# FFN down product of a decoder step as a seven-product Strassen form with standing weights

## What is computed

```python
    y = (jax.nn.silu(gc) * (xn @ w_up)) @ w_down
    return y, gb[:, t:]
...
        yp = yp + f
```

## Time and profile before

| | us |
|---|---|
| median of 3 runs | 2670.74 (2669.45 to 2671.27) |
| the profiled execution | 2667.81 |
| its span, first to last instruction | 2665.9 |
| TensorE busy | 2372.2 (89%) |
| VectorE busy | 1158.6 (43%) |
| ScalarE busy | 675.4 (25%) |
| GpSimd busy | 640.3 (24%) |
| mean granted TensorE clock | 0.953 of full speed |

### The profile page before, as it was taken

The page is one execution under the profiler, slowest core; times in us unless marked ns, Lnnn a source line. Parts: engine busy times, 40 slices in busy tenths (PEclk is TensorE's granted clock), DMA queues, the critical chain, the costliest instruction groups (busy, mean ns, idle before and its releaser), DMA issues. The chain is left out here.

```text
span 2665.9 us, 32803 instructions
## 1 busy us (share of the span) xinstructions
PE 2372.2 (89%) x12653; PEld 1606.8 (60%) x12673; DVE 1158.6 (43%) x2482; ACT 675.4 (25%) x1660; POOL 640.3 (24%) x710
## 2 busy tenths in 40 slices
PE   6999997876888788688779798889999999999999
PEld 4644444553555455455534345458888888878888
DVE  4479997870466566644413112244334433400000
ACT  2321113445455354344401014211111111100000
POOL 1020221113565455456401010022222221100000
PEclk9999997997999899899989899989999999999999
DMA  3211101005899688555430303111111111041100
GB/s 130 72 60 69 37 1 40 1 1 194 303 335 339 242 326 310 180 161 165 118 144 1 110 0 127 64 66 48 33 49 48 33 49 48 18 162 56 58 14 15
DMA packets 125549, 281.75 MB, mean 106 GB/s; under 512 B 14181, under 2 KB 59796, under 8 KB 125396
## 3 DMA queue, kind: packets, MB, share of 16 engines
q0 software_dynamic: 49408, 176.19, 19.5%
q1 hardware_dynamic: 74788, 99.15, 10.9%
q10 hardware_dynamic: 1200, 4.33, 0.4%
HBM read 261.55 MB, written 17.94 MB: 105 GB/s over the span
## 5 line engine op out<-in xcount | busy, mean ns | idle before, releaser
L595 PE MATMUL PS<-X,XT 128*128 128x512 f32 (+5 forms) x864 | 330.5, 538 | 4.3 <-DMA X<-w_in 4.3
L595 PEld LDWEIGHTS PS<-X,XT 128*128 128x128 f32 (+1 forms) x864 | 154.3, 183 | 166.6 <-issue 140.9
L1797 ACT COPY X<-PS 128x512 f32<-128x512 f32 x352 | 193.5, 592 | 213.5 <-PE PS L1678 127.3
L839 DVE TENSOR_SCALAR_CACHE_REDUCE mask<-score,cand 128x384 bf16<-128x384 f32 (+2 forms) x198 | 181.5, 942 | 3.2
L2070 PE MATMUL PS<-dn_w,H 128*128 128x256 f32 x704 | 155.5, 383 | 5.3 <-DMA dn_w<-w_down 5.3
L2070 PE MATMUL PS<-XT,H 128*128 128x256 f32 x704 | 153.3, 380 | 0.0
L2070 PEld LDWEIGHTS PS<-dn_w,H 128*128 128x128 f32 x704 | 134.8, 192 | 25.9 <-DMA dn_w<-w_down 5.7
L2097 DVE TENSOR_TENSOR X<-PS,X 128x256 f32<-128x256 f32 (+1 forms) x36 | 15.2, 423 | 309.4 <-PE PS L2070 308.9
L2070 PEld LDWEIGHTS PS<-XT,H 128*128 128x128 f32 x704 | 133.4, 190 | 19.6 <-issue 0.8
L1550 POOL DMA_INDIRECT XT<-cache_b_v,gather_b x128 | 120.0, 938 | 88.8 <-PE PS L1761 51.4
L1761 PE MATMUL PS<-XT,sa_pt 128*32 128x512 f32 (+1 forms) x1024 | 84.9, 462 | 25.8 <-DMA XT<-cache_b_v,gather_b 19.3
(11 more groups left out here) (408 smaller groups left out, 4415.4 us busy)
## 6 DMA issues: line engine op xcount, KB each, us to landing
ffn_wg<-w_gate SPq DMA_DIRECT2D x11, 1024.0 KB, 5.2
ffn_wu<-w_up SPq DMA_DIRECT2D x11, 1024.0 KB, 5.2
X<-w_in SPq DMA_DIRECT2D x4, 2048.0 KB, 7.8
XT<-w_down SPq DMA_DIRECT2D x2, 2816.0 KB, 16.7
X<-x_prompt ACTq DMA_DIRECT2D x8, 512.0 KB, 7.2
wo_w<-w_out SPq DMA_DIRECT2D x4, 1024.0 KB, 9.6
X<-x_prompt SPq DMA_DIRECT2D x8, 512.0 KB, 13.0
mem_keys<-cache_mem_k SPq DMA_DIRECT2D x8, 512.0 KB, 4.8
```

The source lines that it names most:

```text
L595: last = nc.tensor.matmul(M.PS[0:n, s % 3, 0:chunks[j].width], XT[:, c, t * P:t * P + n], w[:, j % 2, c, 0:chunks[j].width], start=(c == 0 ...
L839: self.link.send(nc.vector.tensor_scalar(self.mask[:, sc], self.score[:, sc], as_float[:, x:x + 1], 0.0, op, ALU.add, accum_out=self.count ...
L1797: nc.scalar.copy(dst, M.PS[0:dst.shape[0], T0 + x % 2, 0:dst.shape[1]]).then_inc(t_read, 1)
```

## The change

`residual_stage` goes and `down_stage` takes its place. Nothing else in the program is changed, except that X and XT are now two parts of one tile named `region`, so that sums of 5808 elements a partition can lie across both.

- The operands change places. Blocks of 11 x 128 x 128 weights stand in the array, and 264 tokens of H move. The 22 feature slices are split into even and odd, the tokens into two halves of 528, and the output columns into pairs of 128. A pair is a 2 x 2 block product, done as seven products in place of eight, each for two pieces of 264 tokens: 14 groups of 11 matmuls to a pair, 4 pairs. The semaphore `mm` counts these groups.
- VectorE makes four sums of H (t1 to t4) once, at the stage's start; t3 is written over a block of H.
- GpSimd makes four sums of weight blocks for each pair: s1 = a21 + a22, s2 = s1 - a11, a21 = a11 - a21, a12 = a12 - s2, each of 1408 elements a partition.
- Weights come as blocks of 128 columns, so in runs of 512 bytes. SyncE issues the four of the first pair; ScalarE issues those of the next pair between its copies.
- Each product block has features on the partitions. TensorE turns it back by five transposes per output quarter (`turn`), 16 turns in all; VectorE adds PSUM to the residual piece in `rest` (`finish`).
- The residual is read from `x_scratch` in pieces of 128 columns, two or three transfers each, and stored the same way; a piece is loaded after the store that used its half of `rest`.

```diff
-def residual_stage(nc, M, K, name, lhs, kc, w_dram, ncol, store=None, spare=None, spilled=None):
...
+def down_stage(nc, io, M, K, H, region):
+    HT = NTOK // 2
+    TW = HT // 2
+    KH = FT // 2
+    PAIRS = KC // 2
+    A, D2, C, TB, TE = 0, 2, 4, 6, 7
...
+        slots = S.sb("w", [P, 6, KH, P])
+        p1, u2, u3, c21 = (S.sb(n, [P, HT]) for n in ("p1", "u2", "u3", "c21"))
+        rest = S.sb("rest", [P, 2, 5, P])
+        t1, t2, t4 = (region[:, k * KH * HT:(k + 1) * KH * HT].rearrange("p (k n) -> p k n", k=KH) for k in range(3))
...
+        t3 = b12
...
+            @block_.sync
+            def _(sp):
+                for i in range(4):
+                    sp.dma_start(block(0, i), weights(0, i)).then_inc(a_loaded[i], 16)
...
+                load(0)
+                load(1)
+                for z in range(4 * PAIRS):
+                    sp.wait_ge(y_done, z + 1)
+                    store(z)
+                    if z + 2 < 4 * PAIRS:
+                        sp.wait_ge(stored[z % 2], 16 * len(stretches(z)) * (z // 2 + 1))
+                        load(z + 2)
...
+            @block_.gpsimd
+            def _(pool):
+                for q in range(PAIRS):
+                    a11, a12, a21, a22, s1, s2 = (block(q, i) for i in range(6))
+                    pool.wait_ge(a_loaded[2], 16 * (q + 1))
+                    pool.wait_ge(a_loaded[3], 16 * (q + 1))
+                    if q:
+                        pool.wait_ge(mm, 14 * (q - 1) + 12)
+                    nc.gpsimd.tensor_tensor(s1, a21, a22, ALU.add).then_inc(w_summed, 1)
+                    pool.wait_ge(a_loaded[0], 16 * (q + 1))
+                    if q:
+                        pool.wait_ge(mm, 14 * q)
+                    pool.wait_ge(w_summed, 4 * q + 1)
+                    nc.gpsimd.tensor_tensor(s2, s1, a11, ALU.subtract).then_inc(w_summed, 1)
+                    nc.gpsimd.tensor_tensor(a21, a11, a21, ALU.subtract).then_inc(w_summed, 1)
+                    pool.wait_ge(mm, 14 * q + 4)
+                    pool.wait_ge(w_summed, 4 * q + 2)
+                    nc.gpsimd.tensor_tensor(a12, a12, s2, ALU.subtract).then_inc(w_summed, 1)
...
+            @block_.tensor
+            def _(pe):
+                def product(bank, left, right, x, begin):
+                    for c in range(KH):
+                        last = nc.tensor.matmul(M.PS[:, bank + x, 0:TW], left[:, c, :],
+                                                right[:, c, x * TW:(x + 1) * TW], start=begin and c == 0,
+                                                stop=(c == KH - 1), skip_group_check=not begin)
+                    last.then_inc(mm, 1)
+
+                def turn(z, src):
+                    if z:
+                        pe.wait_ge(y_done, z)
...
+                        last = nc.tensor.transpose(out, src[:, a - first:a - first + n], K("ident"))
+                    last.then_inc(turned, 1)
...
+                    pe.wait_ge(w_summed, 4 * q + 2)
+                    if q == 0:
+                        pe.wait_ge(x_summed, 2)
+                    for x in range(2):
+                        pe.wait_ge(copied, 6 * q + x + 1)
+                        product(A, s2, t2, x, False)
...
+            @block_.scalar
+            def _(act):
...
+                    for x in range(2):
+                        act.wait_ge(mm, 14 * q + 8 + x + 1)
+                        copy(u3, x, A, copied)
+                    if more:
+                        load_next(q, 2)
+                        load_next(q, 3)
...
+            @block_.vector
+            def _(dve):
+                nc.vector.tensor_tensor(t1, b12, b11, ALU.subtract).then_inc(x_summed, 1)
+                dve.wait_ge(x_summed, 1)
+                nc.vector.tensor_tensor(t2, b22, t1, ALU.subtract).then_inc(x_summed, 1)
+                nc.vector.tensor_tensor(t3, b22, b12, ALU.subtract).then_inc(x_summed, 1)
+                dve.wait_ge(x_summed, 2)
+                nc.vector.tensor_tensor(t4, b21, t2, ALU.subtract).then_inc(x_summed, 1)
...
+                finish(4 * PAIRS - 2)
+                finish(4 * PAIRS - 1)
...
+        region = sb(ctx, "region", [P, NT * D + KC * NTOK])
+        M.X = region[:, 0:NT * D].rearrange("p (t d) -> p t d", t=NT)
+        M.flat = region[:, NT * D:NT * D + KC * NTOK]
...
+        down_stage(nc, io, M, K, H, region)
```

More of the change, by code:

```diff
@@ L2890, in build @@
         Stage.stores = {n: ctx.enter_context(nc.semaphore(n)) for n in (
-            "in_store_done0", "in_store_done1", "kv_store_done0", "kv_store_done1", "ffn_stored0", "ffn_stored1", "dn_stored")}
+            "in_store_done0", "in_store_done1", "kv_store_done0", "kv_store_done1", "ffn_stored0", "ffn_stored1", "dn_stored0", "dn_stored1")}
         M.PS = ctx.enter_context(nc.psum_tensor("PS", [P, 8, 512], F32))
@@ L2896, in build @@
         M.mem_loaded = ctx.enter_context(nc.semaphore("mem_loaded"))
-        M.X = sb(ctx, "X", [P, NT, D])
-        M.XT = sb(ctx, "XT", [P, KC, NTOK])
-        M.flat = M.XT[:].rearrange("p k n -> p (k n)")
+        region = sb(ctx, "region", [P, NT * D + KC * NTOK])
+        M.X = region[:, 0:NT * D].rearrange("p (t d) -> p t d", t=NT)
+        M.flat = region[:, NT * D:NT * D + KC * NTOK]
+        M.XT = M.flat.rearrange("p (k n) -> p k n", k=KC)
         ncst = max(o + w for n, (_, o, w) in const_at.items() if not for_setup(n))
```

156 lines of the change are left out of this document (added).

## The result

| | before | after |
|---|---|---|
| median, us | 2670.09 (2668.34 to 2671.27) | 2635.15 (2632.86 to 2636.51) |
| ratio | | 0.9869, 95% interval 0.9852 to 0.9886 |
| the profiled execution | 2667.81 | 2636.51 |
| its span | 2665.9 | 2634.7 |
| start of the down product | 2338.27 | 2339.42 |

The change is faster by 34.9 us, 1.3%. 28.2 us were forecast, and the time is 1.9 us under the low end of the range. The direction was right, and so was the mechanism in the main; the gain was larger than forecast.

What follows compares the result with a forecast made beforehand. TensorE's matmul columns were taken as the bound: products, clock and turns 287.6 us against 320.8, 33.2 us less; with 0.65 and 4.4 us lost, 28.2 us less. Forecast 2642.5 us, range 2637 to 2652 us.

Steps and rivals of the forecast that it cites:

- The products: TensorE's matmuls in the down product: 1232 records of 0.2225 us, 274.1 us.
- The turns: Five transposes after product blocks: 0.8 us each, 11.2 us for 14; bounds 0.65 and 1.7 us a turn.
- The clock at the start: TensorE's first records in the stage run at a lower clock, costing 2.25 us.
- The start, 0.65 us lost: First weight block of the stage lands at 4.7 us instead of 4.04 us, so TensorE starts 0.65 us later.
- The end, 4.4 us lost: Behind the last product, turn, sums and stores take 7.1 us instead of 2.7 us.
- Rival 1: Stage start: fourth block lands behind 12.65 us, t3 goes first, TensorE waits 5.5 us; 2648.0 us, chance 0.27.
- Rivals 2 and 4: Turns between products: 1.7 us each, about 2657 us, chance 0.08; or they lower TensorE's clock, 2684.4 us, chance 0.03.
- Rival 3: Weights late at each change of pair: three waits of 5 us each, 2657.5 us, chance 0.05.
- The taking of turns between VectorE and GpSimd: Sums at the stage's start: each engine waits for the other's whole instruction; s2 ready at 25.85 us, 0.6 us early.
- The landing of the fourth block, 11.9 us: Last weight block of the first pair lands 11.9 us into the stage, bounds 10.1 to 12.9 us.
- the price of a packet: Weight loads at the stage's start: 28 ns for a packet of 512 bytes, bounds 23 and 31 ns.

Runs made afterwards that it cites:

- e_plain8: The changed kernel with eight block products and no sums in place of seven products: ratio 1.0011 to the kernel before, stage 335.3 us.
- e_turns2: The changed kernel with each turn's five transposes done twice: ratio 0.9916 to the kernel before, stage 304.1 us.
- e_region: The kernel before with X and XT as two parts of one tile and nothing else: ratio 0.9995 to the kernel before, stage 327.4 us.
- a_after: The changed kernel run again, unaltered, on another chip: 2770.45 us against 2804.03 for the kernel before, ratio 0.9868, stage 302.2 us.
- e_late_guard: The changed kernel with the first pair's fourth block issued behind the residual pieces and VectorE waiting for s1 before t3: ratio 0.9884 to before, stage 295.3 us.
- e_split_swap: The changed kernel with the first block in two transfers and s1's product ahead of s2's: ratio 0.9867 to the kernel before, stage 294.1 us.
- e_late: The changed kernel with the first pair's fourth block issued behind the five residual pieces: ratio 0.9883 to the kernel before, stage 302.1 us.

## Why the prediction was off

- **The products**: right. 274.1 us forecast; 283.46 less the turns' 7.6 and the clock's 1.7 leaves 274.2. The price from the FFN stage carried over, and e_plain8 shows the count to be the lever.
- **The turns, "0.65 us for five. I add 0.15 us"**: the step that failed most. They take 0.55 us each, so 11.2 us were forecast for the 14 on the path and 7.6 measured: 3.6 us too dear. The burst of eight in 1.04 us already contained the last record's whole duration; in the chain only the distance between starts counts, 0.11 us, and the break that had 0.15 us costs nothing (e_turns2). The lower bound was the burst's price, so it lay above the truth too.
- **The clock at the start**: 2.25 us forecast, 40.83 - 176 x 0.2225 = 1.7 us measured. 0.6 us less.
- **The start, 0.65 us lost**: 1.3 us. The first block landed 5.34 us after its issue instead of 4.04. 0.65 us more.
- **The end, 4.4 us lost**: 6.43 us against 2.7, 3.7 us lost. 0.7 us less.
- **Sum**: 28.2 + 3.6 + 0.6 - 0.65 + 0.7 = 32.45 us; the profiles show 327.6 - 295.3 = 32.3.
- **The rest**: 34.9 - 32.3 = 2.6 us lie outside the stage. In the profiles of the first result the stage even began 1.15 us later than before, and the medians of the two repeats differ from before by 33.6 and 33.0 us. I take the 2.6 us for scatter; no run shows a cause, and e_region, whose interval reaches to 4.5 us less, does not exclude the single tile as one.
- **The range**: the result lies 7.4 us under the forecast, 4.1 of them from the stage, 2.6 from outside it, and 0.65 since the median of before was 2670.09 us and not 2670.74. The low end was 5.5 us under the forecast. With the turns at 0.55 us the forecast would have been 2638.9 us, and the remaining 3.8 us would have lain within that distance.
- **Rival 1** (chance 0.27) was true in one of the three profiles of the changed kernel; that the profile of the first result was not it hung on 0.8 us, and is luck. 5.5 us was too cheap in sum and too dear in part: s1 and s2 were quicker (3.0 us of work, not 3.5), so the stall was 4.1 us, but I left out the clock that falls behind it, 2.7 us, although the stage's first records priced it. Rivals 2 and 4 are refuted by e_turns2. Rival 3 did not occur: the changed kernel's chain has no gap at any change of pair.
- **The taking of turns between VectorE and GpSimd**: the order was right. The ends came earlier than forecast, s1 at 15.5 us for 16.15, s2 at 24.6 for 25.85, a21 at 33.7 for 35.6, since 1408 elements cost GpSimd 3.0 us and not the 3.5 that come of raising 1.27 us for 512 in proportion.
- **The landing of the fourth block, 11.9 us**: some 11.6 in the first result, 12.7 in a_after, both within the bounds. But the price of a packet rests on a misreading of the window at 134 to 137 us:

```profile
DMA packets 417, 0.14 MB, mean 46 GB/s; under 512 B 288, under 2 KB 416, under 8 KB 416
```

  At most 128 of its packets can have 512 bytes, not 256, and the others are not all tiny, so the 31 ns was no upper bound. That 28 ns came close is luck: from 2341 to 2346 us of the changed kernel 2703 packets of mostly 512 bytes fill 98.0% of the engines' time, 29.0 ns each.

## What to carry to other kernels

If one engine's records bound a stage, the count of its records times their price from a like stage gives the gain well; here most of the error in the stage sat in the bursts between them, whose price is the distance of starts. Where two engines take whole instructions in turn, an event that is late by a microsecond can cost one long instruction (here 6.2 us): look for which large instruction would slip in first, and either make it wait (e_late_guard) or ask for the result later (e_split_swap). Price a stall of the bounding engine with its length and, where it is as long as here (4.1 us), with the clock behind it (2.7 us).

## What the runs showed of the hardware that I had not expected

- A stall of TensorE of 4.1 us brought the clock to the lower level, and the records behind it lost 2.7 us (88 records took 22.31 us in a_after and 22.26 in e_late, 19.58 elsewhere). At the end of the program a wait of 1.1 us did not: the granted clock was 1.00 in the last five transposes, which took 0.75 us.
- The third of four equal weight loads kept SyncE for 3.1 us and the fourth for 2.2, where the four of the kernel before took 0.4 to 1.0 us each. The issues of the changed kernel (ns min/median/max) and their landing:

```profile
L2841 SPq DMA_DIRECT2D dn_w<-w_down x4: 401/1455/3114, 2339.4 to 2343.7; - x4
...
DMA to landing us min/median/max: 5.3/7.1/8.4
```

So the fourth block was issued 4.3 us into the stage, not 1.6. The twice as many runs of 512 bytes are the difference that was made; that they are the cause was not tried.

- Two large sums on VectorE and GpSimd took turns in every profile that has them: t3 and t4 lasted 9.17 us when a GpSimd sum stood before them and 6.21 when none did.
